# The next pair's projection put between the jobs of this pair's solve

## The reference

```python
def project(h, p):
    z = h @ p['w_in'] + p['b_in']                      # h: tokens x 1024
    z_att, z_rwkv, z_gate = jnp.split(z, [ATT_COLS, ATT_COLS + RWKV_COLS], axis=-1)
    ...
    feats = rwkv_features(token_shift(z_rwkv, p['mu_prev'], p['mu_next']), p)

def token_shift(z, mu_prev, mu_next):
    prev = jnp.pad(z[:, :-1], ((0, 0), (1, 0), (0, 0)))
    nxt = jnp.pad(z[:, 1:], ((0, 0), (0, 1), (0, 0)))
    return z + mu_prev * (prev - z) + mu_next * (nxt - z)

def step(S, inp):                                      # once for each token and direction, 8 heads of 64
    r_t, w_t, k_t, v_t, a_t, b_t = inp
    sa = jnp.einsum('bhij,bhj->bhi', S, a_t)
    S = S * w_t[:, :, None, :] + sa[..., None] * b_t[:, :, None, :] + v_t[..., None] * k_t[:, :, None, :]
    return S, jnp.einsum('bhij,bhj->bhi', S, r_t)
```

## Time and profile before

| what | value |
|---|---|
| median of three runs | 3381.65 us |
| the profiled execution: time / span | 3383.62 / 3380.7 us |
| PE busy, matmul | 2728.2 us (81% of the span) |
| DVE, ACT, POOL busy | 1023.0, 769.2, 244.9 us |
| granted TensorE clock, mean | 0.909 of full |
| one turn of the pair loop (second pair, 317.06 to 502.68 us) | 185.62 us |

### The profile page before, as it was taken

How to read it: one execution, slowest core, us unless ns; L and a number is a source line. 1 busy time by engine, 2 the same in 40 slices (tenths; PEclk the granted TensorE clock), 3 DMA queues, 4 the chain that set the end, 5 groups by cost and what they waited for, 6 DMA issues and landing times. The chain is left out here.

```text
span 3380.7 us, 52615 instructions
## 1 busy us (share of the span) xinstructions
PE 2728.2 (81%) x19566; PEld 1401.0 (41%) x19566; DVE 1023.0 (30%) x2428; ACT 769.2 (23%) x1742; POOL 244.9 (7%) x245
## 2 busy tenths in 40 slices
PE   6756666667789996598888988898889499689999
PEld 2444454536476443233322323332333244367444
DVE  1163636354155622311111111111111512555012
ACT  2132322323042002122222222222222201333100
POOL 0040302213000000000000000000000101100000
PEclk9888868878799997699999999999999699786999
DMA  5100000000214622589999999499969421001111
GB/s 188 52 21 6 20 7 20 3 23 4 76 51 161 225 75 105 214 348 373 368 373 380 378 397 372 171 371 398 372 263 369 170 83 59 18 2 50 50 50 75
DMA packets 118953, 569.60 MB, mean 168 GB/s; under 512 B 13808, under 2 KB 17392, under 8 KB 67216
## 3 DMA queue, kind: packets, MB, share of 16 engines
q1 hardware_dynamic: 97184, 510.21, 38.5%
q10 hardware_dynamic: 15472, 36.16, 3.4%
q0 software_dynamic: 6144, 20.98, 1.7%
HBM read 760.50 MB, written 16.52 MB: 230 GB/s over the span
## 5 line engine op out<-in xcount | busy, mean ns | idle before, releaser
L1337 PE MATMUL moe_gu_ps<-expert_w,xgT 128*64 128x512 f32 x3008 | 681.6, 596 | 90.9 <-PEq L1302 90.9
L1337 PEld LDWEIGHTS moe_gu_ps<-expert_w,xgT 128*64 128x64 f32 x3008 | 245.2, 137 | 519.9 <-issue 519.9
L1363 PE MATMUL moe_down_ps<-expert_w,actT 128*64 128x512 f32 x1504 | 348.5, 600 | 67.4 <-PEq L1302 67.4
L1422 DVE TENSOR_TENSOR biased<-moe_gu_ps,b_gu 128x512 f32<-128x512 f32 x94 | 65.0, 692 | 934.7 <-DVEq L1302 934.7
L1363 PEld LDWEIGHTS moe_down_ps<-expert_w,actT 128*64 128x64 f32 x1504 | 114.7, 136 | 240.0 <-issue 240.0
L1547 PE MATMUL pair_z_ps<-hT,x 128*128 128x512 f32 (+1 forms) x384 | 134.1, 515 | 45.9 <-issue 34.6
L1384 ACT ACT_TABLE_LOAD x47 | 60.3, 1283 | 420.9 <-ACTq L1302 420.9
L1266 ACT ACTIVATE xgT<-moe_xg_ps,ffn_shift,ffn_gain 128x64 f32<-128x64 f32 x384 | 119.2, 424 | 42.1 <-PE moe_xg_ps L1260 42.1
L1388 ACT COPY actT<-moe_act_ps 128x256 f32<-128x256 f32 x94 | 35.0, 372 | 400.6 <-ACTq L1302 400.6
L1547 PEld LDWEIGHTS pair_z_ps<-hT,x 128*128 128x128 f32 x384 | 79.2, 207 | 101.8 <-issue 82.1
L386 PE MATMUL b2p_ps<-b_w,b_hT 128*128 128x512 f32 (+1 forms) x320 | 119.4, 535 | 1.9 <-PEq L57 1.9
(11 more groups left out here) (553 smaller groups left out, 3809.6 us busy)
## 6 DMA issues: line engine op xcount, KB each, us to landing
expert_w<-in_w_experts SPq DMA_DIRECT2D x576, 1024.0 KB
late_w<-in_w_late SPq DMA_DIRECT2D x12, 2048.0 KB, 7.7
b_gu<-in_b_experts ACTq DMA_DIRECT2D x96, 256.0 KB
b_w<-in_w_in SPq DMA_DIRECT2D x10, 2048.0 KB, 7.4
ada_w<-in_w_ada SPq DMA_DIRECT2D x6, 2048.0 KB, 12.3
slot_rows<-yb ACTq DMA_DIRECT2D x94, 128.0 KB, 6.2
mix_w<-in_w_in_tok SPq DMA_DIRECT2D x5, 2048.0 KB, 9.7
x<-in_w_rkv SPq DMA_DIRECT2D x5, 1536.0 KB, 6.5
```

Of the source, the lines that this page charges most:

```text
L1337: last = nc.tensor.matmul(ps_gu[SLOTS * j:SLOTS * j + SLOTS, half, :], xgT[:, k, :], w[:, i, at:at + 512], start=(k == 0), stop=(k == KD - 1),
L1363: last = nc.tensor.matmul(ps_dn[SLOTS * j:SLOTS * j + SLOTS, :], actT[:, half, q, SLOTS * a:SLOTS * a + SLOTS], w[:, i, at:at + 512], star ...
L1422: step(nc.vector.tensor_tensor(biased[:, :], ps_gu[:, half, :], b_gu[:, half, :], ALU.add))
```

## The change

The loop runs three turns, and the fourth pair is a written-out copy behind it (`one_pair(3, "last_", False)`). The first pair's projection stands ahead of the loop as before. The projections of pairs 2 to 4 leave their stage: a helper, `ProjectAhead`, puts their 48 products into the solve of the pair before. Eight narrow ones (256 tokens) stand ahead of the first slot, and the other 40 are spread over slots 2 to 54, never more than one ahead of a slot. ACT takes a finished group of eight out behind its own work of a slot; DVE does one operation of the token shift behind some of its slots. The padded rows lie in buffers that are free by then (`bkT_0` and the two `neg`), the PSUM in the two banks that the solve left free. The job `va` moves from first to fifth. The weights of the pair after the next are loaded in the scan stage; a stage `second_w` loads those of the second pair. The solve stage now clears `w_here`, and `pair_output` copies the next pair's columns.

```diff
+        channel_project(nc, "pair_z", w_sb, w_here, [(cols[:, :], d["pair_cols"][0]), (low, d["pair_low"][0])],
+                        hT, lambda i: cols[:, i:i + 1], pair_finish)
+        with stage(nc, "second_w", "none") as (s, block):
+            @block.sync
+            def _(sp):
+                sp.dma_start(w_sb, d["w_rkv"][1]).then_inc(w_here, 16)
...
-        with nc.Fori(0, 4) as pair:
...
+        with nc.Fori(0, 3) as pair:
+            one_pair(pair, "", True)
+        one_pair(3, "last_", False)
...
+class ProjectAhead:
...
+    FIRST, LAST_SLOT = 8, 54
...
+    def ready_by(self, slot):
...
+        if slot >= self.LAST_SLOT:
+            return len(self.todo)
+        return self.FIRST + (len(self.todo) - self.FIRST) * slot // self.LAST_SLOT
...
+    def products(self, pe, s, slot):
...
+        for at in range(self.at, self.ready_by(slot)):
+            i, lo, n, k = self.todo[at]
+            group = at // KD
+            if at == 0:
+                pe.wait_ge(self.w_here, 16)
+            if k == 0 and group >= 2:
+                pe.wait_ge(s["z_kept"], group - 1)
+            last = self.nc.tensor.matmul(self.ps[:, group % 2, 0:n], self.w[:, k, i * P:(i + 1) * P],
+                                         self.hT[:, k, lo:lo + n], start=(k == 0), stop=(k == KD - 1))
...
+    def shift(self, dve, s, slot):
...
+            made = (self.moved // 4 + 1) * 2 * KD
+            if self.moved < 12 and self.ready_by(slot - 4) >= made and slot - 4 >= 0:
+                next(self.moving)
+                self.moved += 1
...
-    jobs = [("va", "act"), ("n", "dve"), ("gb", "dve"), ("q0", "act"), ("gk", "dve"), ("gv", "dve")]
+    jobs = [("n", "dve"), ("gb", "dve"), ("q0", "act"), ("gk", "dve"), ("va", "act"), ("gv", "dve")]
...
             for j, name in enumerate(names):
                 for n in range(3):
                     m = made_of[n]
+                    if ahead:
+                        ahead.products(pe, s, reached(j, n))
                     if j:
                         wait_out(pe, names[j - 1], n)
```

More of the change, by code:

```diff
@@ L1660, in pair_features @@
     with ExitStack() as held:
[L1661 to L1666, removed]
+        ps = held.enter_context(nc.psum_tensor(name + "feat_ps", [P, 4, 1024], F32))
+        one_ka = held.enter_context(nc.sbuf_tensor(name + "one_ka", [P, 1], F32))
+        t1 = held.enter_context(nc.sbuf_tensor(name + "feat_t1", [P, NTOK], F32))
+        t2 = held.enter_context(nc.sbuf_tensor(name + "feat_t2", [P, SEQ], F32))
+        sg = [held.enter_context(nc.sbuf_tensor(name + f"feat_sg{i}", [P, NTOK], F32)) for i in range(2)]
+        with stage(nc, name + "feat", "low", "rates", "squares", "sums", "rooted", "chain", "rk", "bonus", "gate", "gated",
                    "sums_in", "prep", "exped", "one_ka", "kdir") as (s, block):
@@ L1823, in solve_segments @@
     eye = masks[:, 9, :]
-    with nc.psum_tensor("solve_ps", [P, 3, 2, 512], F32) as ps, \
-            stage(nc, "solve", "built_dve", "built_pool", "made0", "made1", "made2", "dve0", "dve1", "dve2",
-                  "act0", "act1", "act2", "aoff0", "aoff1", "aoff2", "chain", "zero") as (s, block):
+    with nc.psum_tensor(name + "solve_ps", [P, 3, 2, 512], F32) as ps, \
+            stage(nc, name + "solve", "built_dve", "built_pool", "made0", "made1", "made2", "dve0", "dve1", "dve2",
+                  "act0", "act1", "act2", "aoff0", "aoff1", "aoff2", "chain", "zero",
+                  *(ahead.SIGNALS if ahead else ()), clear=(ahead.w_here,) if ahead else ()) as (s, block):
         made = (s["made0"], s["made1"], s["made2"])
@@ L1844, in flat, with reached, _ @@
             return t.rearrange("p a q t -> p (a q) t")
-        @block.sync
-        def _(sp):
-            load_next(sp)
+        def reached(j, n):
+            return 3 * j + n + 1
+        if ahead:
+            ahead.made_by = {x: names.index(x) + 1 for x in ("va", "gb", "gk")}
+            @block.sync
+            def _(sp):
+                ahead.load(sp, s)
         @block.tensor
@@ L1993, in _ @@
                         nc.vector.tensor_copy(to, evacuating).then_inc(out["dve"][n], 1)
+                    if ahead:
+                        ahead.shift(dve, s, reached(j, n))
+            if ahead:
+                ahead.shift(dve, s, None)
         @block.scalar
@@ L2015, in _ @@
                             .then_inc(out["act"][n], 1)
+                    if ahead:
+                        ahead.keep(act, s, reached(j, n))
         @block.gpsimd
@@ L2160, in _, with pair_output @@
                     keep_out(k - 1)
[L2163 removed]
+def pair_output(nc, name, g, pair, y, y2, bonus, gate, cols, heads, eps, rwkT, cols_next):
     with ExitStack() as held:
[L2166 to L2169 removed]
+        t = held.enter_context(nc.sbuf_tensor(name + "out_t", [P, SEQ], F32))
+        u = held.enter_context(nc.sbuf_tensor(name + "out_u", [P, SEQ], F32))
+        ps = held.enter_context(nc.psum_tensor(name + "out_ps", [P, 2, 512], F32))
+        with stage(nc, name + "out", "mean", "centred", "squared", "var", "root", "chain", repeats=True) as (s, block):
             @block.tensor
```

132 lines of the change are left out of this document (101 added, 31 removed).

## The result

The changed kernel takes 3317.53 us (median of 4 runs, 3314.85 to 3321.73) against 3382.06 us of the kernel before (4 runs, 3377.27 to 3383.15): ratio 0.982, 95% interval 0.9806 to 0.9834. Taken a second time on another chip it was 3321.12 us against 3382.75, ratio 0.982 (0.9796 to 0.9845). The gain is 62 to 65 us where 20 were forecast.

A forecast was written before the change was run, and what follows sets the result against it. Time was taken as the sum of barrier-separated stages. A pair saves 38.5-30.9+7.9-6.0-0.5-0.6-2.0 = 6.4 us; three give 19.2, plus 2.0-0.9: 20.3 us, so 3361 us; range 3335 to 3385.

The forecast's parts named there:

- What leaves: The projection stages of pairs 2 to 4 go: 115.6 us together, 38.5 us a pair; `second_w` costs 0.9 us once.
- The filling: In the solve, per pair: products fill 1.9 us at the start and 6.0 of 8.5 us of holes, 7.9 us.
- The change-overs: In the solve, 40 lone products each cost 0.15 us at their edges: 6.0 us a pair.
- second rival: In the solve, a change-over costs twice, 0.29 us a product, 11.6 us a pair: 3378 us; chance 0.11.
- The tail: In the solve behind slot 54, PE's 7.1 us of issue waits stay, since no product comes there.
- DVE, ACT and the barrier: In the solve, per pair: 0.5 us for DVE and ACT, 0.6 us for the barrier from clearing `w_here`.
- The job `va`: In the solve, its move from ahead of `n` to behind `gk` is charged nothing, in the last pair either.
- Feat: Feat of pairs 2 to 4 begins with PE at 1.2 GHz: 2.0 us longer a pair.
- Scan, out and the jump: Scan and out were put at no change; reaching the fourth pair without a loop jump saves 2.0 us once.
- first rival: In the solve, holes close wholly (10.4 us) and change-overs are free: 14.9 us a pair, 3336 us; chance 0.2.

The follow-up runs named there:

- e5: Kernel before with `va` moved to fifth, plus 48 extra, unread products of the changed kernel's sizes and slots in all four solves: 3459.3 us, ratio 1.0237.
- e6: Same as e5, but the 48 extra products have 16 columns each: 3391.46 us, ratio 1.0032.
- e7: Changed kernel with its 40 spread products put in five rows of eight, at slots 11, 22, 33, 44 and 54: 3344.46 us, ratio 0.9905.
- e4: Changed kernel with its 40 lone products spread to slot 66 in place of 54: 3313.64 us, ratio 0.9811.
- f3: Changed kernel with its lone products spread to slot 74, the last, in place of 54: 3321.59 us, ratio 0.9823.
- e2: Changed kernel with `va` put back as the first job: 3339.85 us, ratio 0.9888.
- e8: Changed kernel with `va` put back first and the token shift begun only from slot 20: 3323.05 us, ratio 0.9826.
- e3: Kernel before with three loop turns and the fourth pair written out, own projections kept, next weights loaded in scan, `va` first: 3372.95 us, ratio 0.9985.
- f4: Kernel before, unchanged, profiled a second time: 3376.96 us.
- f1: Changed kernel, unchanged, taken a second time: 3321.12 us, ratio 0.982.
- f2: Changed kernel with lone products spread to slot 66 in place of 54, taken again: 3317.24 us, ratio 0.9816.

## Why the prediction was wrong

The sign, the mechanism and most views were right; the gain was three times what was forecast, and the time came out below the range. Of the 41 us by which the loop's sum is off, 12 are holes that were filled and not counted as such, 9 are change-overs, DVE and the barrier charged too high, 5 are feat, 4 the tail, 2 the last solve, and 9 are scans and outs that came out shorter. Step by step:

**What leaves.** Forecast 115.6 us, less 0.9 for `second_w`: 114.7; measured 115.0. `second_w` costs what was forecast: from PE's last product of pair 1's projection to feat it is 6.40 us with it and 5.56 without, 0.84 more.

**The filling: the step that failed most.** The prediction took "70%, 6.0 us" of the 8.5 us of the first three quarters, by an argument on when the next block of instructions is asked for, and 1.9 us at the start. The runs showed the whole of it filled: idle time before `bk` went from 11.9 us to 0.1, 3.9 us a pair more than the 7.9 us forecast. e5 shows it with PE's products alone, and e6 that it needs no long product: 16 columns and their edges close the same holes.

That the holes are waits for instructions, which the prediction took from the packets' number, the traces show in time: all 90 "issue" waits of PE in the eight solves of the two profiles of before end 2.2 to 2.9 us after a 16 KB transfer of the instruction queue began (the wait of 1.61 us that ends at 412.12 behind the one of 409.61). In the solves of the two kernels and of the experiments these transfers never begin less than 3.3 us apart, and some 270 records of PE and its loads lie between two; four small slots, 256 such records, last 2.0 us. The three products in them add 2.4 us by the prediction's sum, enough for the whole of the missing 1.4.

The argument's form was wrong: it let only the half of a block behind the next request count, 1.2 us against a hole of 1.6. The runs fit another reading: a PE that is slowed evenly to the rate at which instructions come has no holes, wherever in the block it is slowed. In e6 the three short products of a block add about 1.3 us, half of which could not close a hole of 1.6, and the holes are all but closed. e7 agrees in part: the same work in lumps leaves 7 to 8 us idle, 2.0 us of it "issue" in pair 2. What makes the requests no closer than that stays open. The Trainium skill (Runtime: NRT & Kernel Launch, Instruction fetch mechanics) calls the cost of these blocks mostly hidden. Here it becomes so once a product stands ahead of most slots; in the kernel before, and in the tail that is left bare, it is not (5.2 us).

**The change-overs.** Forecast 0.15 us each, 6.0 us a pair. Gross, the sizes are the second rival's: 0.31 us around a wide product among small ones, 0.44 us at 16 columns with the product itself, nothing between turns with a wide one. Net, the solve outside its idle pieces grew by 35.0 us (54.5 to 89.5), 4.1 more than the 30.9 us of the products, and the barrier and DVE's share are in that: about 0.10 us a product (the lower clock at the solve's start lasted 3 to 5 us in place of 5 to 7, which helped a little). The three together were forecast at 7.1 us. The second rival took the gross price as a net one. The drain at a change of tiling mode that the Trainium skill states (TensorEngine Tiling (Array Packing), Key Properties) agrees with the gross figures, since only edges to the 64x64 pieces show them; it says nothing on what the edges hide. Term and rival both added edges to filling as if they were independent. They are not.

**The tail.** "Stay" was nearly right: 8.2 us of idle time behind `bk` in the eight solves of before, 7.0 after. With it the solve's 7.8 us a pair are told: 3.9 in the filling, 3.0 in the change-overs with the barrier and DVE, 1.2 here. e4 and f3 show that it could be had too, down to the point where the last shift ends the stage.

**DVE, ACT and the barrier.** Forecast 1.1 us a pair; about 0.7 by the changed kernel against e5. Right in size.

**The job `va`.** "Nothing charged" was right for PE's work and missed DVE's: at its old place the shifts run into POOL's operations, 6.5 us a solve (e2, e8). The prediction looked for what the move does to PE only, and never at where POOL's operations stand. The last pair's solve, 71.9 and 74.0 us after, is no sign of the move: the same written-out code with `va` in front took 71.4 and 75.8 us (e2, e8).

**Feat.** "2.0 us for the lower clock" did not come: the mean feat grew by 0.15 us. The step that failed is the state of the clock in the kernel before: PE came from dense products, but the clock fell by 0.4 us into feat at the latest and was back only 2.9 to 4.4 us in (both profiles), so most of the price was paid already. The prediction's own rows hinted at it: three pairs of products at full clock are 3.9 us, and the sigmoid behind them began at 5.84. Now the clock was back 2.9 to 5.0 us into feat in the loop pairs, and POOL's first operation began 6.7 to 7.7 us into the stage, where it was 6.7 to 7.4 before. Pair 4 of the kernel before, which the prediction took as a sign of the mechanism, had the clock back at 4.4 us and POOL at 7.4.

**Scan, out and the jump.** Scan and out were put at nothing without a reason, though their rows showed a clock of 0.50, and 2.0 us given for the jump. e3 measured 3.3 us for the jump. The remaining 8 us (4.0 in the scans, 4 in the outs) go with a higher granted clock. How much of that belongs to the change and how much to the profiles' moment stays open: f4 and f1 show that either kernel can have either.

The first rival, whose mechanism the runs bear out best (its holes close, though its change-overs are cheap and not free), gave 3336 us. It kept the 2.0 us of feat and the tail as they were, and knew nothing of the clock in scan and out; these make up the rest of the way to 3318.

## What to carry to other kernels

Where an engine stands in the middle of a run of tiny instructions for nothing but issue, other work laid evenly between them costs, as here, little more than what exceeds the holes (30.9 us of products for 22.4 us in e5): spread it, don't lump it, up to where its own followers would end the stage. That last part the solves' lengths show (3.5 us each in f2), the kernel's time not clearly. Don't sum the price of an edge and the filling of a hole; take both from one measurement, such as dummy products in the same places. And when operations move onto DVE, look at what POOL runs at that moment.

## What the runs showed of the hardware that was not expected

- All 90 waits of PE on issue in the solves of before end 2.2 to 2.9 us after the start of a 16 KB transfer of the instruction queue, and such transfers stand at least 3.4 us apart (before, f4).
- Two DVE operations on SBUF, of 0.17 and 0.63 us, took 1.74 us each while POOL ran elementwise operations (e2).
- 48 products of 16 columns, with a longer stretch at 1.2 GHz, add 15.8 us to a solve outside its idle pieces and lengthen the solve by 4.3 us only, since the waits for instructions go (e6).
- In feat of pair 2 the granted clock went from 1.2 to 2.4 GHz after 2.9 us of products one behind the other (3.1 to 5.0 us in the other loop pairs), and back to 1.2 GHz at 351.40, when PE had had no product since 347.23.
- A turn of the loop costs 3.3 us that falling through to written-out code does not (e3).
